# Two shared keys projected as one tile, and constant products placed in TensorE's waits

## What is computed

```
yB = dsa_attention(rope(heads(qB, DSA_HEADS), pos), rope(kB[:, :, None], pos)[:, :, 0], vB,
                   rope(heads(qI, IDX_HEADS), pos), rope(kI[:, :, None], pos)[:, :, 0], wI)
```

## Time and profile before

| | us |
|---|---|
| median of 3 runs | 3052.56 (3048.66 to 3054.7) |
| the profiled execution, its own time | 3046.21 |
| its span, first to last instruction | 3044.3 |
| TensorE busy | 2919.1 |
| VectorE busy | 1560.8 |
| ACT busy | 739.8 |
| POOL busy | 1617.4 |

### The profile page before, as it was taken

One profiled execution on the slowest core, in us unless ns is written; L12 is line 12 of the kernel. 1 busy time (PEld: TensorE's weight loads), 2 busy tenths in 40 slices (PEclk: granted clock), 3 DMA queues, 4 the chain that ended last, 5 costly groups with the idle time before them and its releaser, 6 DMA issues.

```text
span 3044.3 us, 40899 instructions
## 1 busy us (share of the span) xinstructions
PE 2919.1 (96%) x16288; PEld 2328.0 (76%) x16288; DVE 1560.8 (51%) x2929; ACT 739.8 (24%) x1576; POOL 1617.4 (53%) x1126
## 2 busy tenths in 40 slices
PE   7999999999999999999999999999999987899998
PEld 5777777777888877777777778888888677778886
DVE  4663352354887026543433448882252377777711
ACT  3333331112111023343321121111131223311110
POOL 5434555556555664444455565556535164566664
PEclk9999999999999999999999999999999999899999
DMA  6434444445666544444444456765534000355554
GB/s 220 147 131 139 159 145 167 173 145 187 245 240 240 194 156 174 136 136 146 152 166 157 148 180 245 253 243 194 174 132 138 1 3 23 111 171 194 194 193 141
DMA packets 133998, 494.07 MB, mean 162 GB/s; under 512 B 14880, under 2 KB 14880, under 8 KB 132912
## 3 DMA queue, kind: packets, MB, share of 16 engines
q1 hardware_dynamic: 71024, 262.96, 25.7%
q0 software_dynamic: 61200, 222.85, 20.4%
q10 hardware_dynamic: 1584, 5.63, 0.5%
HBM read 489.26 MB, written 2.13 MB: 161 GB/s over the span
## 4 chain that ended last, share of the span: by engine, by line
PE 74%; DVE 9%; issue 8%; POOL 6%; DMA 2%; ACT 1%; POOLq 0%; DVEq 0%; ACTq 0%
PE dense L791 20%; PE dense L793 19%; PE dense L792 19%; POOL raw_lo L2682 4%; PE scores L791 1%; PE scores L1005 1%; PE scores L792 1%; PE scores L793 1%; DMA weights_hi<-stream 1%; PE O L1039 1%; PE O L1073 1%; PE turned L1027 1%; PE dense L1194 1%; PE scores L1059 1%; POOL weights_hi L2672 1%
## 5 line engine op out<-in xcount | busy, mean ns | idle before, releaser
L2682 POOL TENSOR_TENSOR raw_lo<-raw,weights_hi 128x1024 fp32r<-128x1024 f32 x425 | 1021.1, 2403 | 72.1 <-DMA raw<-stream 35.9
L791 PE MATMUL dense<-h_hi,weights_hi 128*128 128x512 f32 x2208 | 884.6, 401 | 16.9 <-DVE h_lo L1870 10.5
L793 PE MATMUL dense<-h_hi,raw_lo 128*128 128x512 f32 x2208 | 865.4, 392 | 0.0
L792 PE MATMUL dense<-h_lo,weights_hi 128*128 128x512 f32 x2208 | 864.1, 391 | 0.0
L2672 POOL DMA_DIRECT2D weights_hi<-stream x425 | 244.8, 576 | 1114.6 <-PE dense L793 1021.3
L791 PEld LDWEIGHTS dense<-h_hi,weights_hi 128*128 128x128 f32 x2208 | 417.2, 189 | 132.6 <-issue 36.5
L793 PEld LDWEIGHTS dense<-h_hi,raw_lo 128*128 128x128 f32 x2208 | 417.0, 189 | 90.4
L792 PEld LDWEIGHTS dense<-h_lo,weights_hi 128*128 128x128 f32 x2208 | 418.0, 189 | 81.6
L791 PE MATMUL dense<-hidden_hi,weights_hi 128*128 128x512 f32 x528 | 205.8, 390 | 2.0 <-POOL raw_lo L2682 2.0
L792 PE MATMUL dense<-hidden_lo,weights_hi 128*128 128x512 f32 x528 | 205.5, 389 | 0.0
L793 PE MATMUL dense<-hidden_hi,raw_lo 128*128 128x512 f32 x528 | 205.5, 389 | 0.0
(11 more groups left out here) (421 smaller groups left out, 4486.0 us busy)
## 6 DMA issues: line engine op xcount, KB each, us to landing
raw<-stream SPq DMA_DIRECT2D x473, 512.0 KB, 3.4
weights_hi<-stream POOLq DMA_DIRECT2D x425, 512.0 KB, 4.6
decays<-stream ACTq DMA_DIRECT2D x8, 512.0 KB, 3.6
gates<-f_scratch SPq DMA_DIRECT2D x2, 1536.0 KB, 8.4
x<-x_in SPq DMA_DIRECT2D x2, 1024.0 KB, 7.4
cond_rows<-cond SPq DMA_DIRECT2D x2, 1024.0 KB, 6.9
dft<-dft SPq DMA_DIRECT2D x4, 512.0 KB, 4.7
out<-x SPq DMA_DIRECT2D x4, 512.0 KB, 2.6
```

Of the source, the lines that this page charges most:

```text
L791: nc.tensor.matmul(to, wh, xh, start=first, stop=False)
L792: nc.tensor.matmul(to, wh, xl, start=False, stop=False)
L793: return nc.tensor.matmul(to, wl, xh, start=False, stop=final)
L2682: nc.gpsimd.tensor_tensor(lo, src, hi, ALU.subtract).then_inc(weights_lo, 1)
```

## The change

The weights of kI and kB become one item, "kIB", with kI in columns 0 to 63 and kB in 64 to 127, so one output of 8 blocks gives both keys, and one pass of rope turns them. ACT then copies the upper half to both halves of kB, and the lower half over the upper one of kI (keys_to_both); the index products wait for the last of these copies. The second run of blocks in pre is `fill(2 * KC + 4)`, 20 blocks, and `fill(2)` stands behind each index product: 56 blocks in the stage.

Products whose results nobody reads are put on TensorE: 42 on a tile of zeros at the very start (it waits for VectorE's memset of the tile), and `idle_products`, with the bfloat16 masks (384 columns) as moving operand: 6 behind norm_stats and 12 behind norm_rows in the four norms of the layers, 24 in the middle of the transposes behind the scan, 8 behind norm_stats(3) and 12 behind residual_rows.

```diff
-            walk(l, ("tok",), ("kI",), order=AFTER_NORM)
-            for p in [("qI", 0), ("qI", 1), ("kB",)] + lead("A", 0):
+            walk(l, ("tok",), ("kIB",), order=AFTER_NORM)
+            for p in [("qI", 0), ("qI", 1)] + lead("A", 0):
...
+            def idle_products(bank, n):
+
+                for _ in range(n):
+                    nc.tensor.matmul(bank[:, 0:3 * P], ident_16, masks[:], start=True, stop=True)
...
-                fill(2 * KC + 6)
+                fill(2 * KC + 4)
...
+                pe.wait_ge(keys_copied, l * 5 + 5)
                 for u in range(DOT_PAIRS):
...
-                    fill(3)
+                    fill(2)
...
+            pe.wait_ge(s_init, 1)
+            for _ in range(42):
+                nc.tensor.matmul(dense[:, 1, :], idle_src[:, 0:P], idle_src, start=True, stop=True)
             pe.wait_ge(s_const, 16)
             for l in range(DEPTH):
                 norm_stats((l, 1))
+                if l == 0:
+                    pe.wait_ge(s_init, INITS)
+                idle_products(dense[:, 1, :], 6)
                 norm_rows((l, 1))
+                idle_products(dense[:, 1, :], 12)
                 pre(l)
...
                 norm_stats((l, 2))
+                idle_products(dense[:, 1, :], 6)
                 norm_rows((l, 2))
+                idle_products(dense[:, 1, :], 12)
...
             for n, t in enumerate(T_ORDER):
+                if n == 2:
+                    idle_products(O, 24)
...
             norm_stats(3)
+            idle_products(turned[:, 0, :], 8)
             residual_stats()
             norm_rows(3)
             residual_rows()
+            idle_products(scores[:, 1, :], 12)
...
+            def keys_to_both(l):
+
+                first, second = slice(0, HEAD_DIM), slice(HEAD_DIM, 2 * HEAD_DIM)
+                act.wait_ge(rope_done, ROPE_NO[(l, "kIB")] + 1)
+                nc.scalar.activation(kB[second, :], kI[second, :], ACT.Copy).then_inc(keys_copied, 1)
+                nc.scalar.activation(kB[first, :], kI[second, :], ACT.Copy).then_inc(keys_copied, 1)
+                act.wait_ge(keys_copied, l * 5 + 4)
+                nc.scalar.activation(kI[second, :], kI[first, :], ACT.Copy).then_inc(keys_copied, 1)
...
+                keys_to_both(l)
                 evacuate((l, "qI", 1))
-                evacuate((l, "kB"))
...
-                rope_cos((l, "kB"))
-                rope_add((l, "kB"))
...
+            nc.vector.memset(idle_src, 0.0).then_inc(s_init, 1)
...
+    if kind == "kIB":
+        return _blocks(np.concatenate([col("kI", 0, 64), col("kB", 0, 64)], 1))
```

More of the change, by code:

```diff
@@ L62 @@
 BEFORE = {"B": "A", "D": "B", "C": "D"}
-ROPED = {"kI", "qI", "kB"} | {(k, b) for k in "q" for b in "BDC"} | {("k", "D"), ("k", "C")}
+ROPED = {"kIB", "qI"} | {(k, b) for k in "q" for b in "BDC"} | {("k", "D"), ("k", "C")}
 TOPK_SPREAD = ([1, 2, 2, 2, 1, 1], [1, 2, 2, 2, 1, 1], [1, 2, 2, 1, 1, 1], [1, 2, 2, 1, 0, 0])
@@ L300 @@
 PREVIOUS_O = {NORMS[n]: NORM_O[p] for n, p in zip(list(NORMS)[1:], list(NORMS))}
-INITS = 5
+INITS = 6
+IDLE_AT = 70
 DENSE_ITEMS = len(DENSE.item_list)
@@ L456, in build_program @@
         tanh_sb, gate_out = region("tanh", TANH_AT)[:, 0, :], region("gate_out", GATE_AT)[:, 0, :]
+        idle_src = region("idle_src", IDLE_AT, 1, BF16)[:, 0, :]
         small = sb("small_sb", [P, SMALL_N])
@@ L604, in build_program @@
             sem(n) for n in ("four_rounded", "four_lo", "gated_rounded", "gated_lo"))
+        keys_copied = f_act
         late_squared, LATE_SQUARED = ab_copied, 2
@@ L829, in operand @@
                     return y_lo[:, k, :], (four_hi, gated_hi)[k // 4][:, k % 4, :]
-                elif kind in ("tok", "kI") or (kind == "up" and e.key[2] == 0):
+                elif kind in ("tok", "kIB") or (kind == "up" and e.key[2] == 0):
                     if l == TAIL:
@@ L1886, in rope_dst @@
                     return qI[:, prod[1], :]
-                if prod[0] in ("kI", "kB"):
-                    return {"kI": kI, "kB": kB}[prod[0]]
+                if prod[0] == "kIB":
+                    return kI
                 if prod[:2] == ("k", "D"):
@@ L1928, in pre @@
             def pre(l):
-                rope_cos((l, "kI"))
-                rope_add((l, "kI"))
+                rope_cos((l, "kIB"))
+                rope_add((l, "kIB"))
                 dve.wait_ge(misc_free, misc_use(l, "tok") + 1)
@@ L1939, in pre @@
                 rope_cos((l, "qI", 0))
-                dve.wait_ge(f_act, l * 2 + 2)
+                dve.wait_ge(f_act, l * 5 + 2)
                 nc.vector.scalar_tensor_tensor(out=logf[:, 3, :], in0=logf[:, 0, :], scalar=0.0, in1=logf[:, 2, :],
@@ L2786, in _ @@
                     issue(w + 1)
-                elif what in (("kI",), ("up", 0, 1)):
+                elif what in (("kIB",), ("up", 0, 1)):
                     low(w)
-                    name = (l, 1) if what == ("kI",) else (l, 2)
+                    name = (l, 1) if what == ("kIB",) else (l, 2)
                     norm_pow(name)
```

6 lines of the change are left out of this document (2 added, 4 removed).

## The result

The changed kernel takes **3023.05 us**, median of 4 executions (3020.26 to 3025.86), the kernel before beside it 3052.98: ratio 0.9913, 95% interval 0.9900 to 0.9926, or 26.6 us less (22.6 to 30.5). Two later groups of runs gave ratios of 0.9912 and 0.9918. The forecast was 3034.6 with a lower end of 3027.0: right in sign and in most mechanisms, too small in size by 8.6 us. The profiled execution took 3025.86 by its own time (before: 3046.21), 20.3 less.

A forecast was written before the change was run, and what follows sets the result against it. TensorE, busy 96% of the span, was taken as the bound. The terms -10.9 + 1.8 - 1.5 - 6.0 - 0.9 - 0.5 = -18.0 us, against the median 3052.56, gave 3034.6 us, range 3027 to 3043.5.

The forecast's parts named there:

- part 1: First stage of each layer: one tile for both keys takes 8 blocks off TensorE per layer; -10.9 us.
- part 2: Same stage: three ACT copies delay qI's evacuation, so TensorE stands 0.9 us per layer; +1.8 us, bounds 0 and 4.2.
- part 3: Index products: two blocks between them instead of three still cover ACT's Relus; 0 us, upper bound 3.6.
- part 4: Kernel start: 42 products on zeros, then 6 and 12 on masks, bring h sooner; -1.5 us, bounds -1.7 and +4.
- part 5: Norms (0, 2), (1, 1), (1, 2): fillers in the gaps save 2.0 us each; -6.0 us, bounds -10 and -3.
- The rule of the Trainium skill: Norm gaps: all shorter than its limit between matmul bursts, so the clock would never have fallen; sum without the norm fillers.
- part 6: Tail: 24 fillers speed the transposes, -0.9 us; norm 3: eight products fill a wait, -0.5 us, bounds -4 and +1.
- the clock up everywhere: Rival, whole kernel: every filled gap is closed and the clock never falls; -25.8 us, 3027, chance 0.20.
- the removed blocks were cover: Rival, first stage: ACT's chain becomes the bound, 10.9 shrinks to about 3; sum -10.5 us, 3042, chance 0.10.

The follow-up runs named there:

- x2: Changed kernel without any of the added products, so the shared key tile alone: 3032.11 us, ratio 0.9954 to the kernel before.
- z4: Changed kernel without the twelve products behind the rows in norms (0, 2), (1, 1), (1, 2) and 3: 3029.31 us, ratio 0.9934.
- w4: Changed kernel run again unaltered, in a later group: 3025.46 us, ratio 0.9918 to the kernel before.
- x4: Changed kernel without the 42 products at the start and the 6 and 12 of the first norm: 3026.29 us, ratio 0.9930.
- y1: Changed kernel run again unaltered, in a later group: 3021.09 us, ratio 0.9912 to the kernel before.
- z3: Changed kernel without the 6 and 12 products of norms (0, 2), (1, 1) and (1, 2): 3025.36 us, ratio 0.9927.
- x1: Kernel before run again, nothing changed: 3048.59 us, ratio 1.0002.

## Why the prediction fell short

1. *One tile* (part 1, -10.9): the blocks' price was right, 9.1 for parts 1 and 2 together against 4.45 + 4.64 = 9.1 in place. The step that failed is the sentence that counts POOL's split and loads at nothing because these engines "are not the bound there". There they are not. But a load less in each layer moves POOL's later pauses against the program, and 3.0 us of TensorE's wait went, with 7 or 8 slow products behind it in two of three traces. The wait stood in the profile of before (PE scores L1005 <- ACT probs L1571, 2.9 us); the prediction does not name it.
2. *The copies* (part 2): 0.63 for 0.60, a stall of 0.47 and 0.65 us for 0.9 each: right, 0.7 too dear. It is not steady: over the traces with the merged tile and the copies ahead of the swap, waits for qI add up to anything from nothing (x2, z4) to 2.5 us (w4).
3. *Index products* (part 3): period 2.2 to 2.6 us, each 0.69 shorter: no wait, as said.
4. *The first stretch* (part 4, -1.5): the 42 took 11.51 us (12 forecast) and are covered. The profiled execution gained nothing, first transposes at 42.55 against 41.71, because after the fillers the clock fell over the dense products, 7 of them from 26.49 us on. Over all traces the transposes start at 41.4 on average in the 12 with these products (8 near 40.8, 4 near 42.5) and at 42.7 in the 6 without: 1.3 us. By the medians x4 is 5 us behind y1, in different groups of runs; the first stretch has no place for more than 1.7 of that.
5. *The three norms* (part 5, -6.0): 4.2 in place, 4.6 by the ratios, inside its bounds. The granted clock decided it, as the earlier trace rows said: the gaps of 1.37 and 2.32 us are back in z3 behind norm (0, 2) (that of 0.66 was never filled), and so are the slow products. The rule of the Trainium skill weighed there ("TensorE: Matmul & The Clock Gate", "Why this matters for your kernels") would have given these fillers nothing; z3 disagrees, by 4.6 us and by a granted clock that falls again.
6. *The tail and norm 3* (part 6, -0.9 and -0.5): the first is 0.6 in place. The second is the mis-sized term: that "forty one-column products follow" and "the clock must fall in them" was false, in most traces it fell behind them (in y1 late_sum's 24 took 2.84 us, the rows 2.05), and the term measures 3.0 in place and 2.4 by the ratios. Its bound of -4 held it, the value taken did not.

With the sizes measured in place the sum is -18.0 - 3.0 (wait in turn D) - 2.5 (norm 3) + 1.8 (middle norms) - 0.7 (copies) + 0.2 (first stretch) + 0.3 (tail) = -21.9, 0.7 short of the near edge of the result's interval (22.6 to 30.5). The other 4.7 us of the 26.6 are tied to no place by these traces, and stay unassigned: that part of the miss is open. The spread of executions is as large: two profiled pairs differ by 20.3 (of which the forecast missed 2.3) and 30.2 (x1 and y1), and the kernel before ranges from 3041.7 to 3055.3 in one group. The range failed with the sum: its lower end was one rival's (the clock up everywhere, -25.8), and nothing in it stood for a gain outside the edited places. One sum of a rival is off as well: in "the removed blocks were cover" 10.9 shrinks to about 3 and parts 4, 5 and 6 add 8.9, which is 12 and not 10.5 (3041 us and not 3042).

## What to carry to other kernels

Fill TensorE's waits where slow work follows and fits: ask for each wait which products behind it run at the lower clock (one-column products count too, 0.1 us each), and size the filler at the upper clock's pace to end just before the releaser. Before costing a removed load at zero, list the long waits that the kernel has anywhere behind it and look for those that follow a pause of the queue itself. Here such a pause moved with the count of loads, and a gain of 3 us came from there that says nothing about the blocks removed. And before a loss is put down to a moved pause, look for it in a run whose pauses stayed. Take the difference of profiled executions with the spread of both kernels around it.

## What the hardware did that I had not expected

- POOL's weights queue pauses about 3 us once in 111 issues: at issue 224 the semaphore update ahead of the load is 2.98 us old at its start (2.29 to 2.98 at 113 in the traces of before and changed, 2.98 at 335 in the changed kernel), elsewhere usually 0.29. Extra issues moved the series to 159, 270 and 381 with the spacing unchanged.
- VectorE's 128x2 operation of L2022 ended with a POOL operation whenever it took longer than 0.16 us, and did not slip in between those that ran back to back: 6.27 us and six times 3.44 to 3.46 in the trace of before beside three of them, 1.09 in the changed kernel beside one, 0.16 with none.
- Slow fillers can be the better outcome. In y1 the twelve of the first norm took 4.05 us and the first dense product came 1.1 us later than in the profile of the changed kernel (23.11 against 22.01), yet the transposes came 1.6 earlier (40.98 against 42.55), for the low stretch lay over fillers and not over dense products.
